# Mixture-of-experts stage of a two-block network: placement in the rounded format, experts gathered two at a time, scatter in four pieces

## The reference, cut to what matters

```
logits = xt @ w_router                      # 256 tokens x 8 experts
top_vals, top_idx = lax.top_k(logits, 2)
combine = one_hot(top_idx) weighted by softmax(top_vals)   # 256 x 8
for e in range(8):
    y = y + combine[:, e:e+1] * ((silu(xt @ w_gate[e]) * (xt @ w_up[e])) @ w_down[e])
```

## Time and profile before

| | us |
|---|---|
| median of 3 runs | 2383.55 |
| profiled execution | 2386.11 |
| its span, first to last instruction | 2384.4 |
| TensorE busy | 2232.1 (94%) |
| VectorE busy | 1762.3 (74%) |
| ScalarE busy | 1326.4 (56%) |

### The profile page before, as it was taken

How to read it: one execution, slowest core, us unless ns; L and a number is a source line. 1 busy time by engine, 2 the same in 40 slices (tenths; PEclk the granted TensorE clock), 3 DMA queues, 4 the chain that set the end, 5 groups by cost and what they waited for, 6 DMA issues and landing times.

```text
span 2384.4 us, 34898 instructions
## 1 busy us (share of the span) xinstructions
PE 2232.1 (94%) x13927; PEld 2002.3 (84%) x13927; DVE 1762.3 (74%) x1952; ACT 1326.4 (56%) x1285; POOL 53.2 (2%) x111
## 2 busy tenths in 40 slices
PE   6899998998989799999898699999999999999997
PEld 4798988998979799999788688888888888888886
DVE  5668956885796555448864588888888888888885
ACT  3464435552534444434443476767676776777674
POOL 5000000000000000000000000000000000000000
PEclk8899999998999899999999799999999999999998
DMA  9945745656543346556343399989999899989992
GB/s 282 192 137 191 253 142 159 189 176 207 171 145 124 106 121 181 176 161 192 100 142 124 118 374 333 374 319 375 342 357 370 325 370 339 369 320 373 340 367 110
DMA packets 414728, 568.82 MB, mean 239 GB/s; under 512 B 16330, under 2 KB 267444, under 8 KB 414576
## 3 DMA queue, kind: packets, MB, share of 16 engines
q1 hardware_dynamic: 410160, 556.31, 68.3%
q0 software_dynamic: 4128, 9.25, 2.1%
q10 hardware_dynamic: 288, 1.05, 0.1%
HBM read 562.37 MB, written 4.19 MB: 238 GB/s over the span
## 4 chain that ended last, share of the span: by engine, by line
PE 79%; DVE 10%; ACT 3%; issue 2%; DMA 0%; ACTq 0%; DVEq 0%
PE pair L1025 58%; PE misc L1025 13%; DVE arena L1904 3%; DVE wlo L1552 2%; PE misc L1425 1%; PE pair L1436 1%; PE misc L1460 1%; ACT whi L595 1%; PE misc L1096 1%; PE misc L1211 1%; DVE rt L1577 1%; PE misc L1337 1%; DVE opl L1570 0%; DVE opf L1609 0%; DVE wlo L2100 0%
## 5 line engine op out<-in xcount | busy, mean ns | idle before, releaser
L2100 DVE TENSOR_TENSOR wlo<-raw,whi 128x2048 fp32r<-128x2048 f32 x338 | 770.1, 2290 | 124.3 <-ACT whi L956 123.4
L956 ACT CAST whi<-raw 128x2048 fp32r<-128x2048 f32 x338 | 646.7, 1917 | 203.3 <-PE pair L1025 101.5
L1025 PE MATMUL pair<-hh,whi 128*128 128x256 f32 x1840 | 533.0, 290 | 27.4 <-DVE hl L1570 19.6
L1552 DVE TENSOR_TENSOR wlo<-raw,whi 128x2048 fp32r<-128x2048 f32 (+1 forms) x174 | 385.2, 2215 | 206.8 <-ACT whi L595 206.2
L1025 PE MATMUL pair<-hl,whi 128*128 128x256 f32 x1840 | 526.9, 286 | 0.0
L1025 PE MATMUL pair<-hh,wlo 128*128 128x256 f32 x1840 | 526.7, 286 | 0.0
L1025 PE MATMUL pair<-whi,oph 128*128 128x512 f32 (+1 forms) x1024 | 394.3, 385 | 4.7 <-DVE wlo L2100 2.9
L1025 PEld LDWEIGHTS pair<-hh,whi 128*128 128x128 f32 x1840 | 359.8, 196 | 34.6 <-issue 29.9
L1025 PE MATMUL pair<-wlo,oph 128*128 128x512 f32 (+1 forms) x1024 | 386.5, 377 | 0.0
L1025 PE MATMUL pair<-whi,opl 128*128 128x512 f32 (+1 forms) x1024 | 385.7, 377 | 0.0
L595 ACT CAST whi<-raw 128x2048 fp32r<-128x2048 f32 (+1 forms) x174 | 320.5, 1843 | 89.1 <-PE pair L1025 60.1
(11 more groups left out here) (411 smaller groups left out, 2492.3 us busy)
## 6 DMA issues: line engine op xcount, KB each, us to landing
raw<-in_moe_w_gate_dram SPq DMA_DIRECT2D x114, 1024.0 KB, 7.2
raw<-in_moe_w_up_dram SPq DMA_DIRECT2D x112, 1024.0 KB, 7.3
raw<-in_moe_w_down_dram SPq DMA_DIRECT2D x112, 1024.0 KB, 6.6
raw<-in_w_in_dram SPq DMA_DIRECT2D x38, 1024.0 KB, 5.3
raw<-in_w_mod_dram SPq DMA_DIRECT2D x24, 1024.0 KB, 5.4
raw<-in_w_up_dram SPq DMA_DIRECT2D x44, 512.0 KB, 5.0
raw<-in_w_xkv_dram SPq DMA_DIRECT2D x16, 1024.0 KB, 5.6
raw<-in_ffn_w_gate_dram SPq DMA_DIRECT2D x22, 512.0 KB, 3.9
```

Of the source, the lines that this page charges most:

```text
L956: act.copy(whi[:, q, :], raw[:, r, :]).then_inc(sem("hi_ready"), 1)
L1025: ins = pe.matmul(out_, lhs, rhs, start=start and i == 0, stop=stop and i == 2)
L1552: dve.tensor_tensor(wlo[:, i_ % SPLIT, 0:size], raw[:, raw_of(n), 0:size], whi[:, i_ % SPLIT, 0:size].bitcast(F32), ALU.subtract).then_inc ...
L2100: dve.tensor_tensor(wlo[:, q, :], raw[:, r, :], whi[:, q, :].bitcast(F32), ALU.subtract).then_inc(sem("lo_ready"), 1)
```

## The change

The tokens (`hn_hi`, `hn_lo`), the placement `place`, `comb_t` and the experts' outputs (`ye_hi`, `ye_lo`) are kept in the rounded format. A gather serves two experts: the two placements stand side by side, so a matmul has 256 columns, and it is made in two passes, of the tokens' high and low parts, into all four `pair` banks. It follows only the second expert of an iteration. The combine weights are no longer in the placement: the plain 0/1 placement is turned, and two one-column matmuls make each slot's weight `weigh_slot`, by which ScalarE scales down's result (`ye_hi`) and VectorE makes `ye_lo`. The scatter is cut into four pieces of four matmuls into `misc` bank 1, in blocks 1, 2, 5 and 6 of the next expert, each behind a turn; each add follows that block's product `sh`. The turn of the last block stands between the two slots of down(5). Zeroing by memset becomes a multiplication by zero.

```diff
+SCATTER_AT = (1, 2, 5, 6)
+        place = ohf[:, 4 * D + 2 * T:4 * D + 4 * T].rearrange("p (i u s) -> p i u s", i=TB, u=2)
+        xg2_hi, xg2_lo = [b[:, 0:2 * D].rearrange("p (u c s) -> p c u s", u=2, s=P) for b in (ohf, olf)]
+        ye_hi, ye_lo = ohf[:, 3 * D:4 * D], olf[:, 3 * D:4 * D]
...
 # ScalarE
+            def gathered_hi(G):
+                for b in range(4):
+                    act.wait_ge(sem("m_x"), G * 4 + (b + 1))
+                    act.copy(xg2_hi[:, 2 * b:2 * b + 2], banks[:, b, :].rearrange("p (c u s) -> p c u s", c=2, u=2)).then_inc(sem("m_xhi"), 1)
...
-                        act.copy(comb_t[:, u], misc[:, 1, 0:T]).then_inc(sem("m_c"), 1)
-                upto(MOE_SLOTS - 1)
-                for half in range(2):
-                    act.wait_ge(sem("m_x"), Q * 2 + (3 + half))
-                    act.copy(xg_hi[1 - u][:, half * 512:(half + 1) * 512], misc[:, 1 - half, :]).then_inc(sem("m_xhi"), 1)
+                        act.copy(comb_t[u], misc[:, 1, 0:T]).then_inc(sem("m_c"), 1)
+                        act.wait_ge(sem("m_yl"), E + 1)
+                        act.copy(weigh_slot[:], misc[:, 1, T:T + 1]).then_inc(sem("m_w"), 1)
+                upto(MOE_SLOTS - 2)
                 hidden_hi(JE - 1)
+                upto(MOE_SLOTS)
+                if u == 1:
+                    gathered_hi(i + (1 + (NE // 2 + 1) * p))
                 upto(MOE_SLOTS + 1)
                 act.wait_ge(sem("slot_used"), E * MOE_SLOTS + (n_split + MOE_SLOTS))
-                act.copy(ye, misc[:, 2:4, :].rearrange("p a b -> p (a b)")).then_inc(sem("m_yc"), 1)
+                act.wait_ge(sem("m_w"), E + 1)
+                act.activation(ye_hi, misc[:, 2:4, :].rearrange("p a b -> p (a b)"), ACT.Copy, scale=weigh_slot[:])\
+                    .then_inc(sem("m_yc"), 1)
...
 # TensorE
+            def gather(G):
+                pe.wait_ge(sem("m_gt"), G + 1)
+                for b in range(4):
+                    for c in range(2):
+                        f = (2 * b + c) * P
+                        for k, part in enumerate((hn_hi, hn_lo)):
+                            for i in range(TB):
+                                ins = pe.matmul(banks[:, b, c * T:(c + 1) * T], part[:, i, f:f + P],
+                                                place[:, i].rearrange("p u s -> p (u s)"), start=(k == 0 and i == 0), stop=(k == 1 and i == 1))
                     ins.then_inc(sem("m_x"), 1)
+            def scatter(r, dst, cb, E):
...
+                for m in range(2):
+                    f = (2 * r + m) * P
+                    pe.matmul(dst[:, m * T:(m + 1) * T], ye_hi[:, f:f + P], comb_t[cb], start=True, stop=False)
+                    ins = pe.matmul(dst[:, m * T:(m + 1) * T], ye_lo[:, f:f + P], comb_t[cb], start=False, stop=True)
+                ins.then_inc(sem("m_s"), 1)
...
                     gate_or_up(j, 0)
                     if j >= 1:
                         turn(j - 1)
+                    if j in SCATTER_AT:
+                        r = SCATTER_AT.index(j)
+                        pe.wait_ge(sem("m_added"), S * 4 + (r + 4))
...
+                        scatter(r, misc[:, 1, :], 1 - u, E + 1)
                     gate_or_up(j, 1)
-                    if j >= 1:
+                    if j == JE - 1:
+                        down(j - 1, (0,))
+                        turn(j)
+                        down(j - 1, (1,))
+                    elif j >= 1:
                         down(j - 1)
                     if j == 3:
                         pe.wait_ge(sem("m_gw"), E + 1)
+                        pe.wait_ge(sem("m_added"), S * 4 + 6)
+                        for i_ in range(TB):
+                            pe.transpose(misc[:, 1, i_ * P:(i_ + 1) * P], place[:, i_, u, :].bitcast(F32), ident[:])
+                        for i_ in range(TB):
+                            ins = pe.matmul(misc[:, 1, T:T + 1], place[:, i_, u, :].bitcast(F32), weigh[:, i_:i_ + 1],
+                                            start=(i_ == 0), stop=(i_ == TB - 1))
                         ins.then_inc(sem("m_ct"), 1)
-                pe.wait_ge(sem("m_c"), E + 2)
-                pe.wait_ge(sem("m_hlo"), E * JE + (JE - 1))
-                gather(Q + 1)
-                turn(JE - 1)
-                scatter(Q, 1 - u, E + 1)
+                if u == 1:
+                    gather(G + 1)
                 down(JE - 1)
...
 # VectorE
+            for q in range(4):
+                part = (slice(None), q // 2, slice((q % 2) * 512, (q % 2 + 1) * 512))
+                dve.wait_ge(sem("h_hi"), DC * NORM["ffn1"] + q + 1)
+                low(hn_lo[part], banks[:, q, :], hn_hi[part], "h_lo")
...
-            dve.memset(ye, 0.0).then_inc(sem("m_yc"), 1)
+            zeroed(ye_hi).then_inc(sem("m_yc"), 1)
+            zeroed(ye_lo).then_inc(sem("m_yl"), 1)
...
                     if j == 2:
-                        placed(place_w, e, True, "m_gw")
-                    if j == 5:
-                        placed(place, e + 1, False, "m_gt")
+                        dve.tensor_copy(weigh[:].rearrange("p (i o) -> p i o", o=1), comb[:, :, bass.ds(e, 1)]).then_inc(sem("m_gw"), 1)
+                    if j == 5 and u == 1:
+                        dve.wait_ge(sem("m_ct"), E + 1)
+                        placed(e + 1, 0)
+                        placed(e + 2, 1).then_inc(sem("m_gt"), 1)
...
                     dve.tensor_tensor(sh[:, j % 2, :], pair[:, j % 2, 1, :], sil[:, j % 2], ALU.mult).then_inc(sem("m_mul"), 1)
-                upto(MOE_SLOTS - 1)
-                for half in range(2):
-                    dve.wait_ge(sem("m_xhi"), Q * 2 + (3 + half))
-                    low(xg_lo[1 - u][:, half * 512:(half + 1) * 512], misc[:, 1 - half, :],
-                        xg_hi[1 - u][:, half * 512:(half + 1) * 512], "m_xlo")
+                    if j in SCATTER_AT:
+                        added(S, SCATTER_AT.index(j), misc[:, 1, :])
                 hidden_lo(JE - 1)
-                added(Q)
+                upto(MOE_SLOTS)
+                if u == 1:
+                    gathered_lo(i + (1 + (NE // 2 + 1) * p))
                 upto(MOE_SLOTS + 1)
+                dve.wait_ge(sem("m_yc"), E + 2)
+                dve.scalar_tensor_tensor(ye_lo, misc[:, 2:4, :].rearrange("p a b -> p (a b)"), weigh_slot[:], ye_hi.bitcast(F32),
+                                         ALU.mult, ALU.subtract).then_inc(sem("m_yl"), 1)
```

More of the change, by code:

```diff
@@ L968, in hidden_hi @@
                     act.wait_ge(sem("m_hT"), E * JE + (j + 1))
-                    act.copy(h_hi[j % 2], misc[:, 1 if j == JE - 1 else 0, :]).then_inc(sem("m_hhi"), 1)
+                    act.copy(h_hi[j % 2], misc[:, 0, :]).then_inc(sem("m_hhi"), 1)
                 for j in range(JE):
@@ L1415, in _ @@
             pe.matmul(misc[:, 0, 16:16 + NE], ones[:], sel[:, 1], start=False, stop=True).then_inc(sem("ranked"), 1)
[L1416 to L1426, removed]
+            pe.wait_ge(sem("h_lo"), DC * NORM["ffn1"] + 4)
@@ L1427, in gather @@
                     ins.then_inc(sem("m_x"), 1)
-            def scatter(S, cb, E):
+            def scatter(r, dst, cb, E):
                 pe.wait_ge(sem("m_yc"), E)
+                pe.wait_ge(sem("m_yl"), E)
                 pe.wait_ge(sem("m_c"), E)
[L1433 to L1437, removed]
@@ L1445, in gate_or_up @@
                         q = (n_split + k) % SPLIT
+                        if j == 0 and kind == 0:
+                            pe.wait_ge(sem("m_xlo"), G * 4 + (2 * half + 2))
                         pe.wait_ge(sem("lo_ready"), E * MOE_SLOTS + (n_split + k + 1))
@@ L1455, in turn, with down @@
                     pe.wait_ge(sem("m_mul"), E * JE + (j + 3))
-                    bank = 1 if j == JE - 1 else 0
-                    if j == JE - 1:
-                        pe.wait_ge(sem("m_xlo"), Q * 2 + 3)
                     for c in range(4):
-                        ins = pe.transpose(misc[:, bank, c * P:(c + 1) * P], sh[:, j % 2, c * P:(c + 1) * P], ident[:])
+                        ins = pe.transpose(misc[:, 0, c * P:(c + 1) * P], sh[:, j % 2, c * P:(c + 1) * P], ident[:])
                     ins.then_inc(sem("m_hT"), 1)
-                def down(j):
+                def down(j, halves=(0, 1)):
                     pe.wait_ge(sem("m_hlo"), E * JE + (j + 1))
@@ L1466, in down @@
                         pe.wait_ge(sem("m_yc"), E + 1)
-                    for half in range(2):
+                        pe.wait_ge(sem("m_yl"), E + 1)
+                    for half in halves:
                         k = (6 * j + 8 if j < JE - 1 else 6 * j + 4) + half
@@ L1479, in moe_expert @@
                 for j in range(JE):
[L1480 to L1487, removed]
+                    pe.wait_ge(sem("m_mul"), E * JE + (max(j, 1) + 1))
                     gate_or_up(j, 0)
@@ L2128, in hidden_lo @@
                     dve.wait_ge(sem("m_hhi"), E * JE + (j + 1))
-                    low(h_lo[j % 2], misc[:, 1 if j == JE - 1 else 0, :], h_hi[j % 2], "m_hlo")
```

(15 more changed lines are left out.)

72 lines of the change are left out of this document (38 added, 34 removed).

## The result

| | before | after |
|---|---|---|
| median, us | 2383.48 (20 runs) | 2370.6 (20 runs) |
| lowest to highest | 2377.87 to 2388.59 | 2363.52 to 2379.25 |
| ratio, 95% interval | | 0.9945 (0.9935 to 0.9955) |
| profiled execution | 2386.11, span 2384.4 | 2367.27, span 2365.5 |

The account below looks back on a forecast made before the run. TensorE's own sequence was taken as the bound, until a slot's subtraction comes too late. Terms: -15.6 over four pairs, +0.7 ahead of the loop, +0.3 after, total -14.6 from 2383.55, giving 2369 us; range 2360 to 2382.

Parts of the forecast that it names:

- Gather: After each second expert: two gathers of 3.57 us become one of 32 matmuls, 3.84 us; net -3.3 a pair.
- Scatter pieces: Behind turns in the next expert: four pieces replace each 3.27 us scatter, net -2.7 a pair; bank and format changes +0.4.
- One-column matmuls: At the placement's turn: two float32 matmuls, four records, cost +0.45 us an expert, +0.9 a pair.
- The stall at slot 40: At down(6) after even experts: the subtraction queued behind hidden_lo comes late, a new stall of 1.1 us.
- rival B: Blocks 1, 2, 4, 5, 6 and the pieces: margins break, 1.7 us a pair of new waits, 2376 us; chance 0.23.
- rival C: ScalarE's scaled copy needs its own table, two loads an expert, 10 us less gain, 2379 us; chance 0.06.
- rival D: At the expert's end VectorE's chain paces the loop, +3.4 us a pair, 2398 us, slower; chance 0.08.
- The loop's turn: Between iterations of two experts: the wait, about 1.0 us, stays, with ScalarE's table load costing 1.28 as before.
- four pair terms: Sum of gather, scatter, placement and stall terms over the experts: -3.9 us a pair, -15.6 for four pairs.
- Ahead of the loop: Before the experts: low-half subtractions +0.3, zeroing +0.6, placements +0.5, first gather -1.4, later cast +0.7; net +0.7 us.
- Third slot's cast: In the first expert: the cast starts behind four short casts, costing +0.7 us.
- After the loop: Behind the last expert: y's low half +1.3 us, scatter and adds shrink from 4.4 to 3.4; net +0.3.

Follow-up runs that it names:

- experiment eight: Changed kernel with slot 40's subtraction ahead of the last block's hidden_lo on VectorE, and the TensorE, ScalarE and VectorE expert loops written out: 2355.68 us, ratio 0.9887.
- experiments two: Changed kernel with the eight experts written out on TensorE instead of a loop, other engines keeping theirs: 2370.83 us, ratio 0.9934.
- three: Kernel before the change with the experts written out on TensorE: 2381.48 us, ratio 0.9993.
- experiment seven: Changed kernel with the expert loops of TensorE, ScalarE and VectorE all written out, subtraction order unchanged: 2360.87 us, ratio 0.99.
- experiment one: Changed kernel with one VectorE edit, slot 40's subtraction ahead of the last block's hidden_lo: 2370.28 us, ratio 0.9938.
- four: Kernel before the change with two unused 1 MB HBM-to-HBM transfers per expert behind the load of slot 5: 2388.81 us, one execution.
- five: Changed kernel with the last block's turn back behind both slots of down(5): 2387.93 us, one execution.

## Why the prediction was right, and where it was not

**What bounds the kernel** was right: time taken from TensorE's own sequence came out of the kernel until a subtraction was late, at the slot named. Transfers at a share of 1.00 never ended a wait for a landing.

**Gather**: 3.84 us once a pair, as worked out. **Scatter pieces**: the slot behind one steps 3.63 instead of 3.08, and the next 2.77 instead of 2.85, so a piece costs 0.47 us in the stream, where 0.48 + 0.05 was taken. **One-column matmuls**: the slot that follows them steps 3.30 instead of 2.86, +0.44 against +0.45. The row of four records in 0.50 us was the right guide; this trace contradicts that they would hide under a weight load. The Trainium skill (TensorE: Matmul & The Clock Gate, section Back-to-back issue gap) gives about 25 ns for each of so few columns; this trace doesn't agree, with 0.44 us for four records.

**The stall at slot 40**: step 3.84 for 2.72, +1.12 against +1.1, and none after an odd expert.

**Expert by expert**, from slot 0 to slot 0: 123 and 125 us in turn were forecast. In after the even experts take 121.6 to 123.2 us and the odd ones 124.0 to 126.9, for an odd one holds the loop's turn at its end; with TensorE's loop written out they take 122.8 to 123.3 and 124.2 to 124.4.

**Thin margins** (rival B): they held. The slot after an add in block 1 has 0.33 us left where it had 0.92, and the one in block 4 0.2. **Scaled copy** (rival C): the loads are still four at each of two lines, and the copy takes 1.12 us instead of 1.02. Here the rule in the Trainium skill (ScalarE: Activation LUTs, section Table sets: the hidden batching unit), cheap functions in every set, agrees with the trace. **VectorE as the pace** (rival D): TensorE's weight loads wait for it 12.3 us over the whole loop (5.7), 5.1 at slot 40 and 5.1 at two of the turns, and these aren't VectorE's. With the first expert it is 13.7, or 3.4 a pair by the profile's label, which is over the 3 us that the prediction set as a sign against itself; without the turns it is 2.2 a pair. VectorE isn't the pace: experiment eight takes TensorE's idle to zero with VectorE busier.

**The loop's turn** is the step that failed: "The wait at the loop's turn stays". It took the wait of about 1 us there for all that the turn costs, and saw only ScalarE's table load behind it. The branch of TensorE was not in the argument at all, because 3.5 us of it lay hidden. Steps at slot 0 of experts 2, 4 and 6 became 4.73, 5.31 and 4.26 (2.0, 2.6 and 1.5 over an unbroken slot), and half clock once added 1.7; the old wait at slot 2 (about 1.1, three times) then had cover. Net +2.0, by experiments two and three: with TensorE's branch out, slot 2 steps 4.20 in the one and 4.10 in the other. The four pair terms themselves, with the branch out, gave 15.2 against 14.9 (15.6 less the 0.7 booked for the third slot of the first expert). So the right total rests on well-sized pair terms and, to a smaller part, on errors that cancel: +2.0 at the turns, +1.2 behind the loop, -1.6 ahead of it.

**Ahead of the loop**: for the two stretches ahead of slot 0 I took +1.4 - 1.4 = 0, and it was -1.6. The four low halves took 2.47 us and went into the wait wholly, zeroing cost 2 x 0.67 less the memset's 0.91, and the placements 0.87 for four. The old gather and what follows it shrank from 8.19 to 6.16 us, where 6.8 was taken. Third slot's cast: +0.7 was taken for standing behind four short casts. The step to slot 2 of the first expert is 3.64 us in after and 2.72 in before, +0.92, but not for that reason. ScalarE in after, then with its loop written out (experiment seven), behind the same four casts:
```profile
1344.38 1.28 ACT L960 ACT_TABLE_LOAD   x1
1345.67 3.71 ACT L960 CAST whi<-raw 128x2048 fp32r<-128x2048 f32 x2
```
```profile
1350.14 1.91 ACT L960 CAST whi<-raw 128x2048 fp32r<-128x2048 f32 x1
```
Without the table load at the loop's head the step is 2.72 again. So the size came out by luck: the casts alone cost nothing, and the load that the sum didn't have here cost 0.9.

**After the loop**: +1.5 instead of +0.3. The chain after the last matmul in after, which answers to the earlier trace rows:
```profile
2335.99 1.11 ACT L1000 ACTIVATE oph<-misc,weigh_slot 128x1024 fp32r<-128x1024 f32 x1 [0.81 <-PE misc L1037]
2337.43 1.28 DVE L2187 SCALAR_TENSOR_TENSOR opl<-misc,weigh_slot,oph 128x1024 fp32r<-128x1024 f32 x1
2338.96 0.36 PE L1449 MATMUL pair<-oph 128*128 128x256 f32 x1 [3.00 <-DVE opl L2187]
...
2342.49 0.69 DVE L2141 TENSOR_TENSOR xT<-pair,xT 128x512 f32<-128x512 f32 x1 [0.16 <-PE pair L1450]
```
The low half cost its 1.3, but TensorE had by then idled 3.00 us; from 2339.3 on its granted clock is 0.50, the scatter's matmuls go 0.21 apart instead of 0.12, and the adds wait for them, 0.85 from one to the next, where 0.66 was counted.

## What to carry to other kernels

Read the sequencer's branches as well as the waits. A loop's turn that costs nothing may be hidden under queued matmuls and a lull of the transfers, and a change that fills that lull puts off its fetch and uncovers it; then a gain elsewhere doesn't arrive (experiment one) until the loop is written out.

Do parts that are each other's cover together, and try a fix of a known stall again when the bigger one is gone: the same one-line swap was worth nothing, and then 4.8 us.

Where an engine is to wait for a short chain across others, place the chain's start one slot earlier and the independent work ahead of its last link.

## What of the hardware was not expected

- TensorE's backward branch takes 3.5 to 3.7 us with transfers at a share of 0.17 to 0.24, and 4.6 to 6.8 us beside transfers that fill the engines. In parts: 1.0 to 1.4 us (2.1 to 4.3 beside transfers) until its packet of 16 KB starts, about 1 for the packet, 1.4 to 1.5 behind it. The branch that falls through takes 0.08. The matmuls already queued covered 4.1 to 4.2 us in after and in experiments one and four, and 3.4 in five.
- After idles of 2.2 to 3.6 us between matmuls TensorE's granted clock often, not always, is 0.50 (1.2 GHz) for 3.4 us: in all three turns of experiment one, in one of three in four (2.31 yes, 2.32 and 2.22 no), and after three of the four idles of 3.60 in five (6.8 us after the first). What decides it isn't shown. Same columns as the earlier trace rows, after:
```profile
1840.90:1844.30 3.40, 3.40 (x8) 2.67 (x9) 1.76 (x2) 1.85 (x1) 0.00 (x0) 0.50 0.94 325
```
  After the idles of 1.84 and 1.38 us at the other two turns of after the clock stays at 1.00.
- One core's transfers hold 362 GB/s over 830 us beside a TensorE that is always busy (experiment eight), and no wait ends with a landing.
- ScalarE's loop costs as well: it has two table loads of 1.28 us in each iteration, and one in all when it is written out. The stream goes from 989.88 to 984.33 us with ScalarE's and VectorE's loops written out too; 5.2 of these 5.5 us are the steps to slot 2 of the even experts (4.20 to 2.77 three times, 3.64 to 2.72 once). A cost of VectorE's own loop isn't seen.
